# Attention by pairs of heads, first two tiles by turns, and weights split by halves, in a kernel of two transformer blocks

## What is computed

```python
def attention_mixer(h, w_qkv, w_o, q_gain, k_gain, cos, sin):      # 16 heads of 64, 4 key heads
    qkv = h @ w_qkv
    q, k, v = jnp.split(qkv, [N_HEADS * HEAD_DIM, (N_HEADS + N_KV_HEADS) * HEAD_DIM], axis=-1)
    q = apply_rope(rmsnorm_2(q, q_gain), cos, sin)
    k = apply_rope(rmsnorm_2(k, k_gain), cos, sin)
    s = jnp.einsum('bqkgd,bskd->bkgqs', q_blk, k) * scale             # for blocks of 128 queries
    p = jax.nn.softmax(s, axis=-1)
    o = jnp.einsum('bkgqs,bskd->bqkgd', p, v)
    return o @ w_o

# first block: h += hybrid_mixer(rmsnorm(h)); h += swiglu(rmsnorm(h))       (528 tokens, 16 of them meta)
# second block, layer 0: attention; layer 1: Hyena. Both:
#   h = rmsnorm_2(x, norm1_g) * (1 + sc1) + sh1;  x = x + g1 * mixer(h)
#   h = rmsnorm_2(x, norm2_g) * (1 + sc2) + sh2;  x = x + g2 * conv_ffn(h)
# at the end: rmsnorm_2(x, final_g)
```

## Time and profile before

| | us |
|---|---|
| median of 3 runs (lowest, highest) | 3399.99 (3398.29, 3401.54) |
| the profiled execution's own time | 3402.33 |
| its span in the profile | 3400.1 |
| PE busy | 3083.2 (91%) |
| POOL busy | 1525.8 (45%) |
| DVE busy | 1417.6 (42%) |
| ACT busy | 720.1 (21%) |
| mean granted TensorE clock | 0.948 |

### The profile page before, as it was taken

The page is one execution under the profiler, slowest core; times in us unless marked ns, Lnnn a source line. Parts: engine busy times, 40 slices in busy tenths (PEclk is TensorE's granted clock), DMA queues, the critical chain, the costliest instruction groups (busy, mean ns, idle before and its releaser), DMA issues.

```text
span 3400.1 us, 38788 instructions
## 1 busy us (share of the span) xinstructions
PE 3083.2 (91%) x14739; PEld 2403.7 (71%) x14739; DVE 1417.6 (42%) x1983; ACT 720.1 (21%) x1069; POOL 1525.8 (45%) x926
## 2 busy tenths in 40 slices
PE   8897899999887999999989889999989777699998
PEld 7885898788634877788866437888867344478886
DVE  5675655111234047433344552332066666433311
ACT  2373222433232000111013551111011111011100
POOL 5441322444203655565543014666555444456663
PEclk9997999999898999999999999999989788899999
DMA  3110000222100245556541002333222000123331
GB/s 111 62 63 32 1 0 0 63 74 74 38 0 25 99 161 182 165 173 188 192 133 62 0 13 62 99 90 102 93 64 101 16 16 16 50 75 99 98 103 59
DMA packets 291644, 259.51 MB, mean 76 GB/s; under 512 B 6329, under 2 KB 263958, under 8 KB 291276
## 3 DMA queue, kind: packets, MB, share of 16 engines
q1 hardware_dynamic: 287840, 248.53, 23.4%
q0 software_dynamic: 2256, 6.55, 0.6%
q10 hardware_dynamic: 1436, 2.96, 0.2%
HBM read 255.92 MB, written 2.10 MB: 76 GB/s over the span
## 4 chain that ended last, share of the span: by engine, by line
PE 78%; DVE 9%; issue 4%; ACT 3%; POOL 2%; DVEq 2%; DMA 1%; POOLq 1%; ACTq 0%; SPq 0%
PE ps L487 19%; PE ps L488 19%; PE ps L489 18%; DVE cv L1881 2%; PE ps L1377 2%; PE ps L1357 2%; PE ps L1453 2%; PE ps L1150 1%; PE ps L1163 1%; PE ps L578 1%; PE ps L1260 1%; PE ps L1169 1%; PE ps L692 1%; DVE HN L598 1%; PE ps L1270 1%
## 5 line engine op out<-in xcount | busy, mean ns | idle before, releaser
L487 PE MATMUL ps<-HNH,spl 128*128 128x512 f32 (+1 forms) x2496 | 914.5, 366 | 61.3 <-DVE HNL L591 24.2
L661 POOL TENSOR_TENSOR spl<-raw,spl 128x1024 fp32r<-128x1024 f32 (+1 forms) x352 | 894.5, 2541 | 55.3 <-issue 5.5
L488 PE MATMUL ps<-HNL,spl 128*128 128x512 f32 (+1 forms) x2496 | 899.3, 360 | 0.0
L489 PE MATMUL ps<-HNH,spl 128*128 128x512 f32 (+1 forms) x2496 | 895.7, 359 | 0.0
L659 POOL CAST spl<-raw 128x1024 fp32r<-128x1024 f32 (+1 forms) x352 | 390.5, 1109 | 1055.0 <-PE ps L489 974.5
L487 PEld LDWEIGHTS ps<-HNH,spl 128*128 128x128 f32 x2496 | 480.2, 192 | 160.9 <-issue 58.6
L488 PEld LDWEIGHTS ps<-HNL,spl 128*128 128x128 f32 x2496 | 480.6, 193 | 72.6 <-issue 4.3
L489 PEld LDWEIGHTS ps<-HNH,spl 128*128 128x128 f32 x2496 | 479.4, 192 | 69.7
L487 PE MATMUL ps<-AFH,spl 128*128 128x512 f32 x528 | 212.8, 403 | 0.0
L489 PE MATMUL ps<-AFH,spl 128*128 128x512 f32 x528 | 205.8, 390 | 0.0
L488 PE MATMUL ps<-AFL,spl 128*128 128x512 f32 x528 | 205.8, 390 | 0.0
(11 more groups left out here) (419 smaller groups left out, 4348.9 us busy)
## 6 DMA issues: line engine op xcount, KB each, us to landing
adw<-in_ada_w SPq DMA_DIRECT2D x96, 512.0 KB, 6.2
raw<-in_w_in SPq DMA_DIRECT2D x44, 1024.0 KB, 5.2
raw<-in_ffn_w_up SPq DMA_DIRECT2D x88, 512.0 KB, 4.8
raw<-in_w_ffn_in SPq DMA_DIRECT2D x44, 512.0 KB, 5.0
raw<-in_ffn_w_down SPq DMA_DIRECT2D x16, 1408.0 KB, 6.4
raw<-in_hy_w_in SPq DMA_DIRECT2D x12, 1024.0 KB, 5.1
raw<-in_w_ffn_out SPq DMA_DIRECT2D x8, 1408.0 KB, 6.8
raw<-in_w_branch_dn SPq DMA_DIRECT2D x8, 1024.0 KB, 5.1
```

The costliest lines, as they stand in the source:

```text
L487: pe.matmul(dst, w[0], x[0], start=first, stop=False)
L488: pe.matmul(dst, w[0], x[1], start=False, stop=False)
L489: return pe.matmul(dst, w[1], x[0], start=False, stop=final)
L661: pool.tensor_tensor(lo, w, hi, ALU.subtract).then_inc(split_ready, 1)
```

## The change

**Norm sums.** For u = 1 to 6 ACT writes the squares of channel blocks 1 to 6 into PSUM banks 1 and 3, and DVE adds them one by one to the square of block 0 (`norm_add`, called in `add_residual`). PE makes two sums per norm: of that total, and of block 7.

**First two tiles by turns.** `pe_first` runs the first two tiles of a GEMM together: for each channel block the three matmuls of tile 0 and the three of tile 1. It stands where `ready` was given: the first projection (u = 0), `ffn_in`, `gq_k`, both `fc_in`, `hy_in`, and the projections `mix_out`, `gq_out` and `hy_out`. It first waits for the first half of both tiles' weights and for both banks.

**Splits by halves.** `pool_split` casts and subtracts the first half of a tile's channel blocks (`gm.mid`), then the second. The first half waits for `acc_half`, which PE raises in the middle of tile t-2, the second for its end. PE waits for `split_first` at a tile's start and for `split_ready` in its middle.

**Attention.** The loop over groups is gone; all is unrolled. Two heads that share a pair of partition halves are one pair, a step e is one block of 128 queries of a pair, 32 steps. Scores and weighted sums of the two heads follow each other in turns. Keys, values and the first two query tiles are made ahead; the other six (`late_tile`) in the middle of the steps, by halves, in bank 7. POOL's copies `qst`, `kst`, `vst` are gone, and the reduction for the maxima is one instruction for both heads. DVE makes the low half of each pair's result from PSUM as soon as it is there.

The diff, cut to its core:

```diff
+        def pe_first(pe, gm, x, ready, wide_t=False):
+
+            pe.wait_ge(split_first, gm.u0 + 2)
+            for t in range(2):
+                pe.wait_ge(acc_free[gm.buf(t)], gm.free(t))
+            for k in range(gm.kt):
+                pe.wait_ge(*ready(k))
+                if k == gm.mid:
+                    pe.wait_ge(split_ready, gm.u0 + 2)
+                for t in range(2):
+                    w, tok, b = halves_of(gm, t, k), x(k), gm.buf(t)
+                    if wide_t:
+                        for h in range(2):
+                            mm = products(pe, ps[:, 2 * b + h, 0:TH], w, [y[:, h * TH:(h + 1) * TH] for y in tok],
+                                          k == 0, k == gm.kt - 1)
+                    else:
+                        mm = products(pe, ps[:, 2 * b, :], w, tok, k == 0, k == gm.kt - 1)
+                    if k == gm.mid - 1:
+                        mm.then_inc(acc_half, 1)
+                    if k == gm.kt - 1:
+                        mm.then_inc(acc_ready, 1)
...
+                if u:
+                    if k in (3, 4, 5, 6):
+                        act.wait_ge(n_add, (KD - 2) * (u - 1) + k - 2)
+                    dst = NSQ[:, k // (KD - 1), 0:n] if k in (0, KD - 1) else ps[:, 1 + k % 2 * 2, 0:n]
+                    act.activation(dst, x(k), ACT.Square).then_inc(n_sq, 1)
+                else:
+                    if k >= 2:
+                        act.wait_ge(n_sum, k - 1)
...
+            act.wait_ge(n_sum, KD + 2 * u)
...
+        def norm_pe(pe, u):
+            pe.wait_ge(n_add, (KD - 2) * u)
+            pe.matmul(ps[:, 6, :], ones[:, :], NSQ[:, 0, 0:SEQ], start=True, stop=False).then_inc(n_sum, 1)
+            pe.wait_ge(n_sq, KD * (u + 1))
+            pe.matmul(ps[:, 6, :], ones[:, :], NSQ[:, 1, 0:SEQ], start=False, stop=True).then_inc(n_sum, 1)
+
+        def norm_add(dve, u, k):
+            dve.wait_ge(n_sq, KD * u + k + 1)
+            dve.drain()
+            x = NSQ[:, 0, 0:SEQ]
+            dve.tensor_tensor(x, x, ps[:, 1 + k % 2 * 2, :], ALU.add).then_inc(n_add, 1)
...
+                    w, hi, lo = gm.view(r)[:, :, m * P:(m + 1) * P], gm.half(u, 0), gm.half(u, 1)
+                    first, second = slice(0, gm.mid), slice(gm.mid, gm.kt)
+                    old = acc_ready if gm.kt > KD and i == 0 and u < 2 else acc_half
+                    pool.wait_ge(old, i * (2 * R) + (gm.u0 + u - 1))
+                    pool.tensor_copy(hi[:, first, :], w[:, first, :])
+                    pool.drain()
+                    pool.tensor_tensor(lo[:, first, :], w[:, first, :], hi[:, first, :], ALU.subtract).then_inc(split_first, 1)
                     pool.wait_ge(acc_ready, i * (2 * R) + (gm.u0 + u - 1))
-                    w, hi, lo = gm.view(r)[:, :, m * P:(m + 1) * P], gm.half(u, 0), gm.half(u, 1)
-                    pool.tensor_copy(hi, w)
+                    pool.tensor_copy(hi[:, second, :], w[:, second, :])
...
+            for gm in (gq_k, gq_v, gq_q):
+                pool_split(pool, gm)
...
+            def q_part(n, bank, ks):
+                gm, t, _ = GQ_TILES[n]
+                if ks[0] == 0:
+                    pe.wait_ge(split_first, gm.u0 + t + 1)
+                    if n < AHEAD:
+                        pe.wait_ge(acc_free[gm.buf(t)], gm.free(t))
+                    else:
+                        pe.wait_ge(a_done, n)
+                for k in ks:
+                    if k == gm.mid:
+                        pe.wait_ge(split_ready, gm.u0 + t + 1)
+                    mm = products(pe, ps[:, bank, :], halves_of(gm, t, k), x_hn(k), k == 0, k == KD - 1)
+                    if k == gm.mid - 1:
+                        mm.then_inc(acc_half, 1)
+                if ks[-1] == KD - 1:
+                    mm.then_inc(acc_ready, 1)
+
+            def v_turn_over(t):
+                taken(pe, gq_v, 0, t)
+                for c in range(NT):
+                    mm = pe.transpose(ps[:, 4 + t, c * P:(c + 1) * P], PTB[:, 0, 0, t, c * P:(c + 1) * P], ident)
+                mm.then_inc(sv_t, 1)
+
+            def scores(e):
+                p, q = e // NT, e % NT
+                if q == 0:
+                    pe.wait_ge(a_done, FIRST_Q + p + 1)
+                if e >= 2:
+                    pe.wait_ge(a_e, 2 * (e - 1))
+                for s in range(2):
+                    x = slice(s * HD, (s + 1) * HD)
+                    mm = pe.matmul(ps[:, e % 2 * 2 + s, :], QG[x, p, q * P:(q + 1) * P], KDUP[x, p // 2, :], start=True, stop=True)
+                mm.then_inc(a_s, 1)
+
+            def turn_over(e):
+                for s in range(2):
+                    i = 2 * e + s
+                    pe.wait_ge(a_p, i + 1)
+                    if i >= 2:
+                        pe.wait_ge(a_tc, i - 1)
+                    for kt in range(NT):
+                        mm = pe.transpose(ps[:, 4 + s, kt * P:(kt + 1) * P], PB[:, e % 2, s, kt * P:(kt + 1) * P], ident)
+                    mm.then_inc(a_t, 1)
+
+            def weighted(p):
+                pe.wait_ge(a_tc, 2 * NT * (p + 1))
+                if p:
+                    pe.wait_ge(split_x, NT + KD + p)
+                for kt in range(NT):
+                    for s in range(2):
+                        x = slice(s * HD, (s + 1) * HD)
+                        mm = pe.matmul(ps[x, 6, :], VG[:, kt, p // 2 * HD:(p // 2 + 1) * HD], PTB[:, p % 2, s, kt, :],
+                                       start=kt == 0, stop=kt == NT - 1)
+                mm.then_inc(a_o, 1)
+
...
+            pe_first(pe, gq_k, x_hn, n_ready)
+            qk_sum(0)
+            pe_tile(pe, gq_v, 0, 0, 0, x_hn)
+            qk_sum(1)
+            qk_rot(0)
+            pe_tile(pe, gq_v, 0, 0, 1, x_hn)
+            qk_rot(1)
+            k_dup(0)
+            q_part(2, 2 * gq_q.buf(0), range(KD))
+            k_dup(1)
+            k_dup(2)
+            q_part(3, 2 * gq_q.buf(1), range(4))
+            qk_sum(2)
+            k_dup(3)
+            q_part(3, 2 * gq_q.buf(1), range(4, KD))
+            qk_rot(2)
             pe.wait_ge(a_dupc, KVH)
             for t in range(2):
-                taken(pe, gq_v, 0, t)
...
+            for e in range(STEPS):
+                p, j, n = e // NT, e % NT, late_tile(e)
+                if e + 2 < STEPS:
+                    scores(e + 2)
+                if j == 0 and p:
+                    weighted(p - 1)
+                if n and j in (1, 2):
+                    q_part(n, 7, range(4 * j - 4, 4 * j))
+                if n and j == 3:
+                    qk_sum(n)
+                turn_over(e)
+                if j == 0 and p and late_tile(e - 1):
+                    qk_rot(late_tile(e - 1))
+            weighted(PAIRS - 1)
+            pe.wait_ge(a_e, 2 * STEPS)
+            pe_gemm(pe, gq_out, lambda k: (OGH[:, k, :], OGL[:, k, :]), lambda k: (split_x, NT + KD + k + 1))
 
...
+            def exps(e):
+                act.wait_ge(a_mx, e + 1)
+                if e >= 2:
+                    act.wait_ge(a_t, 2 * (e - 1))
+                for s in range(2):
+                    act.activation(PB[:, e % 2, s, :], ps[:, e % 2 * 2 + s, :], ACT.Exp, bias=asm[:, e % 2, 1, s:s + 1],
+                                   scale=float(HD) ** -0.5, accum_out=asm[:, e % 2, 2, s:s + 1]).then_inc(a_e, 1)
+
+            def turned(e):
+                p, q = e // NT, e % NT
+                if q == 0 and p >= 2:
+                    act.wait_ge(a_o, p - 1)
+                for s in range(2):
+                    act.wait_ge(a_t, 2 * e + s + 1)
+                    act.activation(PTB[:, p % 2, s, :, q * P:(q + 1) * P], ps[:, 4 + s, :].rearrange("p (k n) -> p k n", k=NT), ACT.Copy)\
+                        .then_inc(a_tc, 1)
+
+            def heads_hi(p):
+                act.wait_ge(a_o, p + 1)
+                act.activation(OGH[:, p, :], ps[:, 6, :], ACT.Copy).then_inc(a_oc, 1)
+
...
+            for e in range(STEPS):
+                p, j, n = e // NT, e % NT, late_tile(e)
+                if n and j == 2:
+                    q_in(n)
+                turned(e)
+                if n and j == 3:
+                    qk_rs(n)
+                if e + 2 < STEPS:
+                    exps(e + 2)
+                if j == 0 and p:
+                    heads_hi(p - 1)
+            heads_hi(PAIRS - 1)
 
             def act_conv_ffn(l, u):
...
+                    if t == KD - 1:
+                        norm_add(dve, u, t - 1)
...
+                    if 2 <= t < KD - 1:
+                        norm_add(dve, u, t - 1)
...
+            def maxima(e):
+                dve.wait_ge(a_s, e + 1)
+                dve.tensor_reduce(asm[:, e % 2, 0, :], ps[:, e % 2 * 2:e % 2 * 2 + 2, :], AX.X, ALU.max)
+                dve.drain()
+                dve.tensor_scalar(asm[:, e % 2, 1, :], asm[:, e % 2, 0, :], -float(HD) ** -0.5, None, ALU.mult).then_inc(a_mx, 1)
+
+            def shares(e):
+                dve.wait_ge(a_e, 2 * e + 2)
```

(23 more changed lines are left out.)

374 lines of the change are left out of this document (145 added, 229 removed).

## The result

The changed kernel takes **3297.68 us** (median of 4 runs, 3296.57 to 3297.99); the kernel before, in the same session, 3399.14 (4 runs). The ratio is 0.9701, 95% interval 0.9684 to 0.9718. The profiled execution took 3296.57 us, so 105.8 less than the profiled one of before, where the prediction's sum took off 81.1.

The account below looks back on a forecast made before the run. PE, busy 91%, was taken as the bound. Attention -47.4, norm sums -28.3, turns -2 + 0.8 + 3.2, splits -4.4 - 3 gave -81.1 us: 3321.2 from the profiled 3402.33, 3319 as median; range 3298 to 3362.

Parts of the forecast that it names:

- the unknown: Attention: whether opposite array halves overlap; taken as yes, three slots instead of four, chance 0.60; without overlap +34 us.
- the prediction's own list: Attention pair with a late tile on PE: scores 5.1, weighted sum 3.84 and other items, 22.7 us with the rope wait.
- some 13 us lower: Attention: the sum if array halves overlapped by a full twofold; kept only as part of the range.
- about as long as PE waited already: Attention's first two tiles: waiting for three halves of late splits would cost PE no more than before.
- the shorter block of DVE: First two GEMMs: shorter POOL subtractions block DVE's convolution taps for less time, -3 us (bounds -6 to +3).
- the earlier starts: Behind the delta rule and at the gate projection: PE starts on one tile's half split, -4.4 us together.
- the wait inside the tile: GEMM tiles: PE's mid-tile wait for the second half of the weights, taken as 0 (bounds 0 to +7 us).
- The term -28.3: Norms behind residuals: 36 sums leave PE at 0.79 us each, in stretches where PE is never idle.
- DVE's cover: Norm sums: DVE's 36 additions of about 0.7 us, one per 5.6 us tile, stay hidden beside PE.
- -2 at the feed-forward inputs: First two tiles by turns: -0.5 us at two feed-forward inputs, -1 at the first, together -2.
- +4 at the output projections: First two tiles by turns: +0.8 us for two output projections, +3.2 for Hyena's, which starts later on its split.
- the bank wait: Feed-forward inputs by turns: tile 0's bank is freed 2.6 us after it is ready, so PE waits until about 2110.0.

Follow-up runs that it names:

- run 1: Changed kernel with a pair's weighted sums made one head after the other instead of alternating: 3314.93 us.
- run 2: Changed kernel with a pair's weighted sums in the order two of one head, two of the other: 3301.38 us, one profiled execution.
- run 4: Kernel before, each weight split made in four short instructions instead of two, nothing started or freed earlier: 3387.66 us, ratio 0.9966.
- run 6: Kernel before with only the splits by halves, including starts and buffer frees by halves: 3383.68 us, ratio 0.9956.
- run 8: Changed kernel with the first two tiles one after the other again, each waiting for its own split: 3295.13 us, ratio 0.9704 to the kernel before.
- run 7: Changed kernel with norm squares summed on PE again, eight sums a norm, none on DVE: 3326.57 us.
- run 3: Changed kernel with every weight split whole again, buffers freed at a tile's end and PE waiting for the whole tile: 3348.64 us.
- half tiles in turn: Changed kernel with all first tile pairs ordered first half of tile 0, first half of tile 1, then the second halves: 3286.07 us.

## Why the prediction was wrong in size, point by point

**Attention, the step that failed.** The price of the unknown: "If halves run at once, but starts stay in order ... scores 1.28 us per step", nine steps for a weighted sum. Starts don't stay in order (runs 1 and 2). Scores took 0.86 and the change, weighted sums 3.42 and the change. By the prediction's own list a pair loses 1.7 + 0.4 = 2.1 of its 22.7 us and is 20.6: exactly what was measured. Six such pairs are 12.8 of the 24.7 us missing between the profiles; the last two add 2, the first turn 1.9, the stretch ahead of the loop 0.8, and 1.2 us that stood between the last sum and `gq_out` are gone: 18.7 in all. The rule of the Trainium skill ("TensorEngine Tiling (Array Packing)": tiles run in parallel by Key Properties, up to twofold by Theoretical Speedup) had the right size, and I had named it as "some 13 us lower" but kept it out of the sum. The other rule there, that a change of form drains, cost nothing beyond the 0.17 to 0.2 us a change that the prediction counted. Against this, PE starts the key tiles 3.1 us later than before, and Hyena's input 2.2 later, since it waits for the first halves of two tiles' weights; the sum had put that at 0 ("about as long as PE waited already").

The 0.3 us by which the median lies outside the range say little, since the clock gives or takes 2.8 us in one stage (last section). The 21 us by which the point value was off are far above that.

**Splits by halves: mechanism right, size wrong.** Both effects were in the text, the shorter block of DVE at -3 (bounds -6 to +3) and the earlier starts at -4.4. Measured alone, the short block is worth 13 us by the medians (15 by the profiles), 10.7 of it in the first two GEMMs. The mis-sized term is "-3 for the first two GEMMs together"; they lost 9.3. In `dn_v` PE gave back 4.8 us over 16 tiles, the 0.2 to 0.3 per tile of the forecast. The sum lacked `dn_qk`: the forecast expected it to pay for its late start, and it won 3.0 (6.6 in run 4, where its waits for ScalarE's copy went), and 1.5 more went between the two. The sum also put at 0 the stretch ahead of `mix_out`, which lost 3.5 (0.7 with pieces alone in run 4, 3.7 with the frees in run 6), and the Hyena input, which lost 5.6: 2.0 with pieces alone; tile by tile (run 8) it takes 144.4 us, no less than before, so the rest goes with the turns and with PE's later start. The early starts failed at the gate projection: the wait inside the tile, taken as 0, was 1.76 and 1.78 us there, since PE had caught up with POOL. In steady GEMMs it was 0: their tile period stayed 5.56 us.

**Norm sums: mechanism right, the price of one too low.** The term -28.3 is 36 times 0.79 us; a sum costs 0.90 (run 7), which makes 32 to 33. Two runs that differ in the sums and in attention alone, 6 and 8 (both tile by tile, both with halves), differ by 32.1 us over the six stages with sums. That is about 4 of the 24.7 us. The lines of the sums fell from 96 records to 24, as forecast, and DVE's cover held. `mix_out` won another 1.4 us already in run 6: PE's wait for ScalarE's first square, 2.0 us before, is 0.6 there.

**Turns: nearly nothing in total, as summed (+2.0), but by other places.** The forecast had -2 at the feed-forward inputs and +4 at the output projections. The convolutional inputs lost 2.7 us each in the changed kernel's profile: the bank wait was foreseen, but tile 0's reader was taken to start 12.0 us behind PE and started 13.5 behind it, and nine matmuls ran at the lower clock again after the wait. With another clock the same inputs lost nothing (last section). The output projections themselves lost 0.5 or less against run 8. At `hy_out` PE started 6.0 us after POOL's first cast in place of 3.6, +2.4 against 3 forecast. At the qkv input the turns won 3.9 (run 8).

**The parts together.** Four profiles make steps from the kernel before to the changed one. The splits by halves take off 18.3 us (before to run 6). Attention by pairs and the sums take off 88.1 (run 6 to run 8): 54.2 from the down projection's end to `gq_out`, 2.8 less than it might be for the clock at the loop's end, and 32.1 in the six stages with sums; 1.8 are left over. The turns add 0.9 (run 8 to the changed kernel). Together that is -105.5, the difference of the spans. The 66.1 of attention's stretch in the table has the turns' 3.9, the halves and the later start in it, and can't be added to the rest.

**Not settled:** why the taps of `dn_qk` are slower with whole splits behind turns (run 3) than with whole splits before, and why the clock falls in some executions and not in others.

## What to carry to other kernels

Two independent matmuls that claim half the array each should stand close together in the program: alternating them, or going by twos, took the whole time of one away (3.58 and 3.63 us for 16 records); four of one ahead of four of the other took 5.35. Where two engines block each other per instruction, make the long instruction of the one with slack short, even if its total grows: that alone took 13 us off the kernel before. And when two tiles take turns, look at what both release at the same moment: finish one of them early (half tiles in turn), and free its inputs in pieces. Price an instruction by tiles of the GEMM it is taken from: the sum's 0.79 came from a tile of another GEMM, and 36 times the difference was 4 us.

## What the runs showed of the hardware

**A half of TensorE's array starts work past waiting instructions of the other half.** In run 1 a record started ahead of three earlier ones; with eight records of one head ahead of the other's eight, four of twelve steps were shared. That is read from the number of records that start at each step; the trace doesn't name a record's head.

**A wait can bring the clock down or not, at the same place of the program.** Behind the third tile's wait of 1.94 us the changed kernel's profile shows nine matmuls 0.34 to 0.43 us apart (granted 1.2 GHz), then 0.23 (2.4 GHz). In run 1 the same wait is followed by 0.23 at once:

```profile
2035.74 0.47 PE L486 MATMUL ps<-HNH,spl 128*128 128x512 f32 x1 [1.94 <-DVE SG L2376]
```

That input took 251.45 us in the one and 248.65 in the other. PE's first matmuls behind the norm differ too, 14 at the lower clock against 10. So 2.8 us in such a stage prove no edit: with turns and early frees the two inputs took 248.7 to 251.5 us over the runs, tile by tile 249.0, and only the 246.9 of half tiles in turn lies outside. That the turns lose there is open; that half tiles win is shown, by 1.8 to 4.6 us each. The end of the attention loop is a second such place (run 8): 2.8 us again.

**The same tap took 0.77, 0.87, 1.16, 1.54 or 2.65 us.** The 2.65 stood beside a subtraction of 1024 columns and the 1.54 beside one of 512; the others are not traced to their causes.
